# One wait taken out of the load queue of a hybrid attention and mixture-of-experts block

## The chip, the cores and the metric

The kernel runs on one core of a Trainium2 chip. The metric is the device time of one execution in microseconds; lower is better. Times inside an execution come from the hardware profiler and are counted from the start of its span.

## The reference

One transformer block on 512 tokens of width 2048, all in fp32. Three kinds of attention (differential, forgetting, and a compressed/selected/windowed one) are computed and projected by `w_out`, and the result is added to x. Then comes a hierarchical mixture of experts:

```python
g_prob = jax.nn.softmax((xt @ wg) + bg)                 # 8 groups
g_p, g_idx = lax.top_k(g_prob, 1)                       # one group per token
e_val, e_loc = lax.top_k(e_in, TOP_K_EXPERTS)           # 2 of the group's 8 experts
...
return (jax.nn.silu(xc @ w_gate[e]) * (xc @ w_up[e])) @ w_down[e]
...
x = x + hier_moe(h, ...)
return rms_norm(x, ln_f)
```

There are 64 experts; each has gate and up weights of 2048 x 256 and down weights of 256 x 2048, so three matrices of 2 MB (2048 KB) each, 384 MB (192 matrices) for all.

## The kernel before, in words

The first half of the execution is attention and the output projection. The sum x2 (x plus the attention's part) is stored to a scratch tensor in DRAM, transposed for the router, and the router's logits are made (`add_logits`, L1203).

The second half goes through the experts one by one, in 8 groups of 8. For a group the tokens that chose it are gathered as rows from the scratch tensor into `xg[g % 2]` by an indirect DMA that GpSimd issues (`gather`, L859; for the first group L865). VectorE builds a 0/1 matrix `pick` (L2170) that says which row goes to which slot of which expert, and TensorE multiplies the gathered rows by it (`pick_half`, L1285); ScalarE and VectorE copy the product to `xT`. The group's first four experts come from `pick_half(g, 0)`, the last four from `pick_half(g, 1)`. For each expert TensorE then runs `gate_up` (L1363 and L1364), a transpose (L1373), `down_product` (L1388) and `spread_result` (L1334), which adds the weighted result to the group's rows.

The weights come over SP's DMA queue (q1 in the profile). SP walks down a fixed list, `LOAD_ORDER`, and waits in front of each load for the buffer's last user. Load n has a number: 0 and 1 are gate and up of expert 0, 2 and 3 of expert 1, 4 is down of expert 0, 5 and 6 are gate and up of expert 2, 7 is down of expert 1, 8 is gate of expert 3, and so on. There are eight 16 KB-per-partition buffers that are used over and over (`chunk`). Load 6, the third expert's up weights, is alone: it is made once into two places of 8 KB per partition, `xg[1]` (where the second group's rows come later) and `lnf_sb` (where ln_f comes later), in two halves. Load 8 (L787) is issued ahead of load 6, and load 7 (L794) goes into the space of the transposed x2, so it waits for `logits_ready`. Loads 9 to 12 are made in quarters, each after TensorE's `gate_up` of expert 0 or 1 has read that quarter of the old contents (`load_quarters`, L747). From load 13 on each waits for TensorE to be done with the buffer (`chunk_used`, `load_chunk`, L734).

The gather is on GpSimd's own queue (q0 in the profile). TensorE's `pick_half(0, 0)` waits for both `pick_ready` and `xg_in[0]`, the gather's landing. Until then TensorE is kept busy by multiplications that nobody reads (`keep_busy`, L1240).

Of the kernel before, what the change touches and what calls it, by code (L numbers as in the profile page):

```python
# [351 lines left out]
def hybrid_block_moe_kernel(nc, x_in, ln1, w_in, diff_lambda, diff_subln, fox_bf, cmp_pos_k, cmp_w1_k,  # L352
# [3 lines left out]
    with ExitStack() as ctx:  # L356
# [6 lines left out]
        def sem(name):  # L363
            return ctx.enter_context(nc.semaphore(name))
# [246 lines left out]
        g_copied, xg_in, out_landed = sem("g_copied"), [sem(f"xg_in{b}") for b in range(2)], sem("out_landed")  # L611
# [45 lines left out]
        def _(sp):  # L657
# [73 lines left out]
            def load_chunk(n):  # L731
                e, kind = LOAD_ORDER[n]
                s = slot_of(n)
                sp.dma_start(chunk[s], sources[kind][:, e, :]).then_inc(ex_in[s], 16)  # L734
# [50 lines left out]
            sp.wait_ge(x2_transposed, 4 * NT)  # L785
            sp.wait_ge(row2_sum, NT * NT)
            load_chunk(SLOTS + len(ONCE) + 1)  # L787
            sp.wait_ge(xg_in[0], 16)
            for k in range(2):
                half = slice(k * KT // 2 * D_EXPERT, (k + 1) * KT // 2 * D_EXPERT)  # L790
                e, kind = LOAD_ORDER[ONCE[0]]
# [117 lines left out]
        def _(pe):  # L909
# [226 lines left out]
            for n in range(ALL_STEPS):  # L1136
                if n > 0:
                    fill(n, 0)
                fill_out(n)
                filled = any(lo < hi for _, lo, hi, _ in filling(n, 0))  # L1140
                if filled:
                    transpose_probs(n)
                if n >= 1:
                    values(n - 1)
                if not filled:
                    transpose_probs(n)
                fill(n, 1)
                if n + LOOK < ALL_STEPS:
                    scores(n + LOOK)
# [300 lines left out]
        def _(act):  # L1450
# [153 lines left out]
            def take_turns(n, half):  # L1604
                for tile, _, _, turns in filling(n, half):
                    if turns:
                        take_turned(tile)
# [14 lines left out]
            def turn_next(n):  # L1622
                return n < ALL_STEPS and any(turns and lo == KT for _, lo, _, turns in filling(n, 0))
# [741 lines left out]
```

## Time and profile before

| | us |
|---|---|
| median of 3 runs | 1950.96 |
| lowest and highest run | 1949.98, 1952.01 |
| span of the profiled execution, first to last instruction | 1948.3 |
| median less span | 2.7 |

| engine | busy us | share of the span |
|---|---|---|
| TensorE (PE) | 1871.1 | 96% |
| VectorE (DVE) | 702.2 | 36% |
| ScalarE (ACT) | 585.3 | 30% |
| GpSimd (POOL) | 245.5 | 13% |

The profile lists no separate time for the profiled execution; the 2.7 us are what lies between its span and the median of the runs. "Busy" counts an engine's own instructions; a DMA is seen in the columns for bytes per microsecond and in the time from its issue to its landing. A row of a timeline that ends with a bracket says how long the engine was idle before it and who released it.

### The profile page before, as it was taken

How to read it: one execution, taken by the hardware profiler on the slowest of the kernel's cores; microseconds unless marked ns; L12 is line 12 of the kernel's file. 1: busy time of each engine (PE TensorE's matmuls, PEld its weight loads, DVE VectorE, ACT ScalarE, POOL GpSimd, SP SyncE). 2: the span in 40 equal slices, each digit the busy share in tenths (PEclk: the TensorE clock that was granted, in tenths of full speed). 3: DMA queues.
4: the chain of work that ended last, by engine and by line, in shares of the span. 5: the costliest groups of instructions: out<-in, count | busy, mean ns of one | idle time of the engine just before them, and what ended most of it. 6: DMA issues, size and time to landing. Idle time of an engine off the chain costs nothing.

```text
span 1948.3 us, 28600 instructions
## 1 busy us (share of the span) xinstructions
PE 1871.1 (96%) x11936; PEld 1351.5 (69%) x11936; DVE 702.2 (36%) x1773; ACT 585.3 (30%) x1212; POOL 245.5 (13%) x208
## 2 busy tenths in 40 slices
PE   6999999999999999999999999989999899999996
PEld 5887777777777777788986656556565565655663
DVE  4331223333766668701142232322323123232322
ACT  5323333333543444422312231313213131121322
POOL 2433343333000000144100000000000000000000
PEclk9999999999999999999999999999999999999998
DMA  9553233233222231146499999999999999999994
GB/s 280 142 149 113 71 82 87 65 77 86 53 68 44 56 125 70 44 144 206 191 369 411 428 427 427 426 426 428 426 427 429 426 428 426 427 427 427 427 427 197
DMA packets 177393, 505.95 MB, mean 260 GB/s; under 512 B 52834, under 2 KB 136162, under 8 KB 151146
## 3 DMA queue, kind: packets, MB, share of 16 engines
q1 hardware_dynamic: 174954, 495.66, 66.4%
q0 software_dynamic: 2304, 8.39, 1.1%
q8 instruction: 97, 1.59, 0.3%
q14 instruction: 38, 0.31, 0.0%
HBM read 495.88 MB, written 16.53 MB: 263 GB/s over the span
## 4 chain that ended last, share of the span: by engine, by line
PE 79%; DMA 18%; ACT 1%; DVE 1%; issue 0%; SPq 0%; POOL 0%; POOLq 0%; ACTq 0%; DVEq 0%
PE banks L955 26%; PE banks L1363 12%; DMA at_region<-in_w_up 10%; PE banks L1112 9%; DMA x_region<-in_w_up 8%; PE banks L1388 7%; PE banks L1285 6%; PE banks L1364 3%; PE banks L1092 3%; PE banks L1064 2%; PE banks L1042 2%; PE banks L1334 2%; PE banks L1004 1%; PE banks L1203 1%; PE banks L1049 1%; PE banks L1373 1%
## 5 line engine op out<-in xcount | busy, mean ns | idle before, releaser
L955 PE MATMUL banks<-ht_rounded,ring_rounded 128*128 128x512 f32 x1056 | 359.3, 394 | 0.7 <-ACT at_region L1526 0.7
L955 PEld LDWEIGHTS banks<-ht_rounded,ring_rounded 128*128 128x128 f32 x1056 | 195.2, 188 | 53.5 <-issue 13.8
L1363 PE MATMUL banks<-at_region,ht_region 128*64 128x256 f32 x800 | 185.5, 392 | 13.3 <-DMA at_region<-in_w_up 13.3
L852 POOL TENSOR_TENSOR ring_rounded<-ring_region,at_rounded 128x512 fp32r<-128x512 f32 (+1 forms) x92 | 116.0, 1292 | 509.4 <-ACT at_rounded L1465 509.4
L1364 PE MATMUL banks<-at_region,ht_region 128*64 128x256 f32 x768 | 180.1, 395 | 0.0
L2257 DVE SCALAR_TENSOR_TENSOR at_rounded<-banks,small,ring_rounded 128x512 fp32r<-128x512 f32 x128 | 96.0, 750 | 208.4 <-ACT ring_rounded L1751 207.5
L1363 PEld LDWEIGHTS banks<-at_region,ht_region 128*64 128x64 f32 x800 | 112.1, 142 | 74.4 <-issue 27.7
L2250 DVE COPY consts<-banks 128x128 f32<-128x128 f32 x64 | 18.6, 291 | 397.9 <-PE banks L1373 397.9
L1751 ACT ACTIVATE ring_rounded<-banks,small 128x512 fp32r<-128x512 f32 x128 | 88.0, 688 | 240.1 <-PE banks L1388 240.1
L955 PE MATMUL banks<-ht_rounded,at_rounded 128*128 128x512 f32 x352 | 142.7, 405 | 1.0 <-ACT at_region L1518 0.7
L1741 ACT ACTIVATE ring_region<-banks,consts 64x256 f32<-64x256 f32 x64 | 30.1, 470 | 368.7 <-PE banks L1364 368.5
L955 PE MATMUL banks<-mix_rounded,at_rounded 128*128 128x512 f32 x352 | 137.6, 391 | 0.0
L955 PE MATMUL banks<-mix_rounded,ring_rounded 128*128 128x512 f32 x352 | 137.5, 391 | 0.0
L852 POOL TENSOR_TENSOR ring_rounded<-ring_region,ring_rounded 128x512 fp32r<-128x512 f32 x88 | 111.2, 1296 | 199.2 <-ACT ring_rounded L1465 199.2
L1112 PE MATMUL banks<-ring_rounded,ht_rounded 128*128 128x512 f32 x384 | 129.9, 392 | 0.0
L1285 PEld LDWEIGHTS banks<-ring_region,mix_region 128*128 128x128 f32 x512 | 116.7, 306 | 15.8 <-issue 12.2
L1285 PE MATMUL banks<-ring_region,mix_region 128*128 128x256 f32 x512 | 125.0, 399 | 0.0
L1363 PE MATMUL banks<-x_region,ht_region 128*64 128x256 f32 x480 | 107.9, 384 | 8.1 <-DMA x_region<-in_w_up 7.2
L1364 PE MATMUL banks<-x_region,ht_region 128*64 128x256 f32 x512 | 115.5, 384 | 0.0
L882 POOL DMA_INDIRECT out<-mix_region,g_idx x8 | 8.1, 1007 | 837.3 <-DVE mix_region L2267 837.3
L1364 PEld LDWEIGHTS banks<-at_region,ht_region 128*64 128x64 f32 x768 | 108.6, 143 | 0.0
L1363 PEld LDWEIGHTS banks<-x_region,ht_region 128*64 128x64 f32 x480 | 65.9, 138 | 45.6 <-issue 18.6
(300 smaller groups left out, 3473.7 us busy)
## 6 DMA issues: line engine op xcount, KB each, us to landing
at_region<-in_w_gate SPq DMA_DIRECT2D x24, 2048.0 KB, 29.8
at_region<-in_w_up SPq DMA_DIRECT2D x23, 2048.0 KB, 28.2
at_region<-in_w_down SPq DMA_DIRECT2D x22, 2048.0 KB, 24.4
ring_region<-in_w_in SPq DMA_DIRECT2D x36, 1024.0 KB, 6.0
x_region<-in_w_down SPq DMA_DIRECT2D x17, 2048.0 KB, 27.4
x_region<-in_w_up SPq DMA_DIRECT2D x15, 2048.0 KB, 30.0
x_region<-in_w_gate SPq DMA_DIRECT2D x14, 2048.0 KB, 30.2
ring_region<-in_w_gate SPq DMA_DIRECT2D x9, 2048.0 KB, 33.1
```

What stands on the lines that cost most here:

```text
L852: ins = nc.gpsimd.tensor_tensor(w_low[n % RING][:, ks, 0:width], ring[n % RING][:, ks, 0:width], w_high[n % 2][:, ks, 0:width].bitcast(F32 ...
L955: ins = mm(out, w[:, k, 0:width], h[:, k, :], start=k == 0 and i == 0, stop=k == KT - 1 and i == 2)
L1042: ins = mm(S[:, par, half, 0:W], q[pr][rows, cols], keys[kind == "win"][rows, 0:W], start=True, stop=True)
L1064: ins = nc.tensor.transpose(PT[:, half, kb * P:(kb + 1) * P], probs[:, n % 2, half, kb * P:(kb + 1) * P], ident)
L1092: ins = mm(o, v[:, kb, cols], pT[:, half, j * P:(j + 1) * P], start=kind == "fox" and kb == 0, stop=part != "slc" and kb == qb)
L1112: ins = mm(out, a[:, 4 * c + i, t * P:(t + 1) * P], b[:, i, :], start=first and i == 0 and k == 0, stop=last and i == 3 and k == 2)
L1285: mm(place[turn[j]][:, 0:HALF], rows[:, j, :], slots, start=True, stop=True).then_inc(picked, 1)
L1363: mm(place[0:CAP, 0:D_EXPERT], x, gate[j], start=j == 0, stop=j == KT - 1)
L1364: ins = mm(place[CAP:2 * CAP, 0:D_EXPERT], x, up[j], start=j == 0, stop=j == KT - 1)
L1388: ins = mm(PT[side * CAP:(side + 1) * CAP, m, :], hidT[:, j, :], down[:, j, (2 * side + m) * T:(2 * side + m + 1) * T], start=j == 0, stop ...
L1751: fn(y_high[:, m, :], PT[:, m, :], ACT.Copy, scale=own_weight[e8 % 2]).then_inc(y_a, 1)
L2257: v.scalar_tensor_tensor(y_low[:, m, :], PT[:, m, :], own_weight[e8 % 2], y_high[:, m, :].bitcast(F32), ALU.mult, ALU.subtract).then_inc(y ...
```

## The change

SP no longer waits for the landing of the first group's gathered rows (`xg_in[0]`) before it issues the two halves of load 6. Nothing else is changed.

```diff
             load_chunk(SLOTS + len(ONCE) + 1)
-            sp.wait_ge(xg_in[0], 16)
             for k in range(2):
                 half = slice(k * KT // 2 * D_EXPERT, (k + 1) * KT // 2 * D_EXPERT)
                 e, kind = LOAD_ORDER[ONCE[0]]
                 sp.dma_start(second_gate[k], sources[kind][:, e, half]).then_inc(once_in, 16)
             sp.wait_ge(logits_ready, 1)
             load_chunk(SLOTS + len(ONCE))
```

## Rows read from the trace of the kernel before

**Rows 1.** The page, chain of work that ended last, shares of the span.
```profile
PE 79%; DMA 18%; ACT 1%; DVE 1%; issue 0%; SPq 0%; POOL 0%; POOLq 0%; ACTq 0%; DVEq 0%
```

**Rows 2.** Stretches: length, then PE, PEld, DVE, ACT, POOL busy, clock, DMA share, GB/s.
```profile
982.00:986.00 4.00, 4.00 (x31) 3.96 (x30) 1.24 (x5) 0.47 (x1) 0.00 (x0) 1.00 0.34 86
...
1044.00:1051.00 7.00, 7.00 (x63) 4.68 (x64) 0.76 (x2) 0.47 (x1) 0.00 (x0) 1.00 1.00 424
1051.00:1054.00 3.00, 3.00 (x24) 1.52 (x22) 0.97 (x4) 0.47 (x1) 0.00 (x0) 1.00 0.66 213
1054.00:1224.00 170.00, 170.00 (x1222) 107.34 (x1220) 48.17 (x109) 40.19 (x74) 2.25 (x3) 1.00 1.01 427
1224.00:1926.00 702.00, 663.21 (x4644) 425.24 (x4642) 193.40 (x429) 163.04 (x300) 12.22 (x16) 0.98 1.00 424
```

**Rows 3.** The chain in order of time, second half: start us, us, what.
```profile
984.70 7.39 PE banks L1285 x32
...
1224.50 25.34 DMA at_region<-in_w_up
```

**Rows 4.** Waits of TensorE from 984 to 1220 us, all of them.
```profile
PE banks L1388 <- issue: 0.4, 1, 0.4
```

**Rows 5.** Timeline of SP's queue: start us, us, line, operation.
```profile
965.30 0.33 SPq L734 DMA_DIRECT2D mix_region<-in_w_gate  x1
984.15 0.33 SPq L792 DMA_DIRECT2D mix_region<-in_w_up  x1
...
985.00 0.43 SPq L734 DMA_DIRECT2D ht_region<-in_w_down  x1
994.94 0.33 SPq L747 DMA_DIRECT2D at_region<-in_w_up  x1
...
1051.75 0.33 SPq L734 DMA_DIRECT2D at_region<-in_w_down  x1
```

**Rows 6.** Timeline of all engines around the first gather.
```profile
972.44 0.19 DVE L2106 TENSOR_TENSOR at_region<-banks,small 128x32 f32<-128x32 f32 x1 [11.29 <-PE banks L1203]
...
978.76 1.17 POOL L865 DMA_INDIRECT mix_region<-x_scratch,idx_i  x1 [42.53 <-issue]
...
983.81 0.69 DVE L2170 TENSOR_TENSOR ring_region<-consts,small 128x512 f32<-128x512 f32 x1
...
984.55 7.54 PE L1285 MATMUL banks<-ring_region,mix_region 128*128 128x256 f32 x32
```

**Rows 7.** DMA view of 978 to 990, 1749 to 1763, 1940 to 1949 us.
```profile
q0 software_dynamic: 144, 0.44, 12.5%
...
mix_region<-x_scratch,idx_i POOLq DMA_INDIRECT x1, 5.4
...
q0 software_dynamic: 145, 0.16, 3.1%
...
mix_region<-x_scratch,g_idx POOLq DMA_INDIRECT x1, 10.3
...
q0 software_dynamic: 144, 0.16, 5.1%
...
out<-mix_region,g_idx POOLq DMA_INDIRECT x1, 3.8
```

**Rows 8.** DMA view of 986 to 990 and 1040 to 1050 us: packets by size.
```profile
DMA packets 205, 1.55 MB, mean 387 GB/s; under 512 B 16, under 2 KB 16, under 8 KB 16
...
DMA packets 292, 4.26 MB, mean 426 GB/s; under 512 B 32, under 2 KB 32, under 8 KB 32
```

**Rows 9.** TensorE after two idle times: timeline rows and stretches (columns as above).
```profile
1491.99 0.40 PE L1363 MATMUL banks<-mix_region,ht_region 128*64 128x256 f32 x1 [2.34 <-DMA at_region<-in_w_up]
...
1492.00:1495.00 3.00, 3.00 (x28) 2.44 (x30) 1.63 (x1) 0.00 (x0) 0.54 (x1) 1.00 1.03 437
...
1418.51 0.66 PE L1363 MATMUL banks<-at_region,ht_region 128*64 128x256 f32 x1 [2.49 <-DMA at_region<-in_w_up]
...
1418.40:1421.60 3.20, 3.09 (x16) 1.99 (x18) 0.00 (x0) 0.00 (x0) 0.00 (x0) 0.50 1.00 425
1421.80:1425.00 3.20, 3.20 (x32) 2.33 (x30) 0.00 (x0) 0.00 (x0) 0.00 (x0) 1.00 1.01 430
```

## The prediction, made before the changed kernel ran

> **What bounds the kernel now.** I read the page's chain first: 79% of the span on TensorE and 18% on DMA [rows 1]. Such shares are a mean over stages, so the next view is the table of stretches [rows 2]. From 1054 us almost to the end the DMA engines move 424 to 427 GB/s with no gap. From 1054 to 1224 us TensorE is busy for all of its 170 us as well; after 1224 us it is busy for 663 of 702 us and waits for weights. The chain says the same: it stays on TensorE from the first picking at 984.70 us until, at 1224.50 us, the first DMA stands in it [rows 3]. So the last 700 us go at the pace of the weight stream, and what matters is when that stream becomes unbroken, and who sets that moment.
>
> The stretches show it: from 1044 to 1051 us the stream runs at 424 GB/s, from 1051 to 1054 us only at 213 [rows 2]. SP's queue shows why: a load is issued at 1051.75 us [rows 5], for a buffer that TensorE has just freed, and the queue ahead of it had run dry. From there on it never does again. And TensorE, from 984 to 1220 us, has one wait of 0.4 us [rows 4]: it runs back to back from the first `pick_half`. Hence the rule that I use: **the end of the kernel moves by as much as TensorE's start on `pick_half(0, 0)` moves**. A transfer that arrives earlier between 984 and 1051 us only makes the dry moment before 1051.75 us longer.
>
> What releases that start at 984.55 us? Two things, almost at once [rows 5, 6]. VectorE's `pick` is done at 983.81 + 0.69 = 984.50 us. The gather was issued at 978.76 us and landed 5.4 us later [rows 7], at about 984.15 us, which is when SP, waiting for the same landing, went on [rows 5]. So the gather has only some 0.35 us of slack.
>
> **The change, part by part.** *What is moved.* SP had issued load 8 at 965.30 us and then stood until 984.15 us [rows 5]. Now the two halves of load 6 follow at about 965.7 and 966.1 us, 18.5 us earlier. Load 7, behind them on SP, waits only for the logits, which TensorE finishes as VectorE is released at 972.44 us [rows 6]; it goes out at about 972.5 instead of 985.00 us, 12.5 us earlier. Behind it come the quarters of loads 9 to 12; the first is issued at 994.94 us [rows 5] after `gate_up` of expert 0 has read its quarter, so they stay tied to TensorE. GpSimd's queue isn't changed: the gather is still issued at 978.76 us.
>
> *What is gained.* From 982 to 986 us the stream was almost empty, 86 GB/s [rows 2]: a hole of (427 - 86) x 4 = 1364 KB, 3.2 us of stream. It is now filled. By the rule above that buys nothing, since no one waits for loads 6 or 7 before 1051 us [rows 4]: they were in time already. Value: 0. If it did reach the end, it would be worth up to 3.2 + 0.9 (the ramp from 986 to 990 us at 387 GB/s, 160 KB or 0.4 us, and the hole's edges, about 0.5) = 4.1 us; that is the lower bound, and a rival below.
>
> *What is lost.* The gather used to travel as load 8 ran out. Now 4.2 MB more lie in SP's queue when it starts: 9.8 us at 427 GB/s, so the stream is full until about 992 us, beyond any time at which the gather could land. What does an indirect DMA cost beside a full stream? The nearest rows are two of one size, 0.16 MB each [rows 7]: alone, at the end of the kernel, 3.8 us; beside the stream, 10.3 us. The stream costs 6.5 us. The gather has 144 packets, 9 for each of the 16 engines. Packets of the stream are 16 KB where a row of 16 KB is loaded: from 1040 to 1050 us 292 less 32 small ones carry 4.26 MB, 16.4 KB each [rows 8], which at a sixteenth of 427 GB/s is 0.61 us. The 6.5 us are then 10.6 such packets: about one ahead of each of the gather's nine and one or two more at the start. But load 6 goes into two places of 8 KB per partition, and its packets are half as large: from 986 to 990 us 205 less 16 small ones carry 1.55 MB, 8.2 KB each [rows 8], 0.31 us. The gather meets the tail of load 8 and then load 6, which alone fills 4.9 us. So 10.6 x 0.31 = 3.3 us, plus 0.3 us for one packet of load 8 ahead of it. The gather itself, alone, with 0.44 MB: 3.8 + 0.28 MB / 427 GB/s = 4.5 us. Sum: 4.5 + 3.3 + 0.3 = 8.1 us, landing at 986.9 us. TensorE starts 2.4 us later than 984.55 us.
>
> The bounds of this term: below, 5.4 us as now, a delay of 0. Above, all of the stream priced as 16 KB packets: 10.3 + 0.7 = 11.0 us, landing at 989.8 us, a delay of 5.3 us. I take 2.4 us since the packets' size is what the rows say of this very load.
>
> The Trainium skill, in DMA: Bandwidth & Descriptors, "Queues, rings and completion order", says that each DMA engine goes round its queues and changes only at packet boundaries. By that alone, nine stream packets for nine of the gather's, the sum would be 4.5 + 9 x 0.31 = 7.3 us and the delay 1.6 us; no row here shows the order of single packets. The same page's fit in "Anatomy of one DMA", about 2 us plus the bytes at 436 GB/s, would price the gather at 3.0 us beside anything, and the change at nothing; the trace disagrees with 10.3 us for 0.16 MB.
>
> *TensorE's clock.* TensorE would now be idle for about 2.3 us between the end of its kept-busy work and `pick_half`. The trace has idle times on both sides of what that does [rows 9]: after 2.34 us the granted clock stayed at 1.00 (2.4 GHz); after 2.49 us it was 0.50 (1.2 GHz), and 16 matmuls ran in 3.2 us where 32 ran afterwards: 1.6 us lost. At 2.3 us I take it as not falling, 0, and keep 1.6 us for the range.
>
> *Everything else* follows TensorE and shifts with it: the marks on VectorE, the quarters, the second gather. The instructions removed cost nothing.
>
> Sum: 0 + 2.4 + 0 = **+2.4 us**; the span 1948.3 becomes 1950.7, and with the 2.7 us that the median lies above the span, **1953.4 us**. A measurement of this kernel can tell about 0.2% (3.9 us) from no change, so this is a loss that would count as none.
>
> **Rivals.** *A, the forecast with a fallen clock.* The same delay a little longer, and 1.6 us for the clock: 1950.96 + 2.4 + 1.6 = 1955.0 us, just past 0.2%. For it: 2.3 us of idling stands directly at 2.34 and 2.49 us. Against: the idle time is spread over only one row of each kind, and picking is also paced by copies.
>
> *B, the stream costs the gather its full price.* Packets already taken in by the engines, or load 7 being met as well, make it like the later gathers: 5.3 us of delay and 1.6 us of clock, 1957.9 us. For it: the smallest indirect DMA beside the stream took 10.3 us [rows 7]. Against: the 8 KB packets.
>
> *C, nothing happens.* The gather finishes nearly as fast as now, within its slack of 0.35 us or a microsecond of it: 1951.0 to 1952 us. For it: the present 5.4 us already contain over 2 us beside load 8. Against: 10.3 against 3.8 us.
>
> *D, faster.* The hole of up to 4.1 us is the weight stream's own time, and that stream sets the pace of the last 700 us. If the load at 1051.75 us were not tied to TensorE, or TensorE's start did not move and something before 1051 us was short of weights, the end would come up to 4.1 us earlier, 1946.9 us. It decides at the dry moment: the stream must be unbroken through 1051 to 1054 us. Against it: 213 GB/s there, and TensorE's single wait of 0.4 us [rows 2, 4].
>
> **How the numbers follow.** Forecast with the clock kept 0.40; A 0.22; B 0.17; C 0.13; D 0.08. The forecast's own range is 1952.3 to 1954.8 us. The range from C's 1951.0 less a microsecond of spread between runs to near B: 1950.0 to 1957.6 us. Slower by over 0.2% is B and most of A: 0.34. Faster by over 0.2% is D alone, at its full price: 0.07. The rest, 0.59, is the same.
>
> **What the changed profile would show.** SP issues the two halves near 965.7 us and load 7 near 972.5 us. No stretch from 978 to 990 us falls below 400 GB/s; the stream runs dry between about 992 us and the first quarter instead. The gather's time to landing is 8.1 us. TensorE has a wait for it in front of L1285 of about 2.3 us, with the clock beside it. The first quarter is issued near 997.3 us, and the load now at 1051.75 us near 1054.2 us, again with the stream dry before it. The prediction is wrong if L1285 starts on time, if the wait is over 4 us, or if the stream shows no gap near 1054 us.

## The result and the profile after

The changed kernel takes 1956.07 us (median of 10 runs, 1953.17 to 1957.19) against 1951.57 us for the kernel before in the same runs (1949.98 to 1952.74). The ratio is 1.0022, with a 95% interval from 1.0013 to 1.0031: 4.3 us slower, and the interval excludes no change. It lies in the predicted range of 1950.0 to 1957.6 us; the predicted step was 2.4 us, and the line of 0.2% on which the chances were cut runs through the measured interval, so whether the loss is above or below it isn't decided.

The profiled execution took 1956.5 us, with a span of 1954.6 us. All that lies ahead of the router came about 1.1 us later in it than in the profile of before (the gather is issued at 979.83 instead of 978.76 us), which has nothing to do with the change. So times are best read as distances from the issue of the gather. The lines of `kernel.py` behind the removed one have moved up by one: L1284 here is L1285 of before.

SP's queue, the rows that answer to [rows 5] (start us, us, line, operation):

```profile
966.35 0.33 SPq L734 DMA_DIRECT2D mix_region<-in_w_gate  x1
966.72 0.43 SPq L791 DMA_DIRECT2D mix_region<-in_w_up  x1
...
973.41 0.33 SPq L734 DMA_DIRECT2D ht_region<-in_w_down  x1
1001.34 0.33 SPq L747 DMA_DIRECT2D at_region<-in_w_up  x1
...
1058.15 0.33 SPq L734 DMA_DIRECT2D at_region<-in_w_down  x1
```

Load 6 follows load 8 at once, and load 7 went out with the logits. But the first quarter and the load that was at 1051.75 us are later, not earlier.

Stretches of the changed kernel (columns as in [rows 2]):

```profile
982.00:986.00 4.00, 3.77 (x42) 3.57 (x42) 2.16 (x7) 0.20 (x1) 0.00 (x0) 1.00 1.01 412
986.00:990.00 4.00, 0.64 (x3) 0.67 (x4) 0.00 (x0) 0.00 (x0) 0.00 (x0) 1.00 1.05 434
...
994.00:996.00 2.00, 2.00 (x10) 2.00 (x10) 1.18 (x3) 0.95 (x2) 0.00 (x0) 1.00 0.00 0
996.00:998.00 2.00, 2.00 (x10) 2.00 (x10) 1.15 (x3) 0.95 (x2) 0.00 (x0) 1.00 0.00 0
998.00:1000.00 2.00, 2.00 (x26) 1.77 (x26) 1.54 (x4) 0.47 (x1) 0.00 (x0) 1.00 0.00 0
...
1057.00:1060.00 3.00, 3.00 (x26) 1.66 (x24) 0.97 (x4) 0.47 (x1) 0.00 (x0) 1.00 0.91 333
```

The hole of before, 86 GB/s from 982 to 986 us, is filled: 412 GB/s. It has come back at 994 to 1000 us, where nothing moves at all. In its place TensorE is idle from 985.8 to 989.4 us. The dry moment in front of the later load is still there, at 1057 to 1060 us, but it is shallower: over the three microseconds that begin 0.75 us ahead of that load's issue the stream runs at 317 GB/s, against 213 before [rows 2].

The one of TensorE's waits from 940 to 1400 us that lies in front of the first picking, then the chain that ended last, in order of time (start us, us, what), and TensorE's stretches right after its wait:

```profile
PE banks L1284 <- DMA mix_region<-x_scratch,idx_i: 3.6, 1, 3.6
```

```profile
979.83 9.40 DMA mix_region<-x_scratch,idx_i
...
989.36 9.12 PE banks L1284 x32
```

```profile
990.30:993.60 3.30, 3.30 (x10) 2.58 (x9) 0.97 (x2) 1.03 (x3) 0.00 (x0) 0.50 0.69 293
993.70:997.00 3.30, 3.30 (x17) 3.30 (x16) 1.77 (x4) 1.60 (x4) 0.00 (x0) 1.00 0.01 5
```

The gather, 5.4 us long before [rows 7], takes 9.4 us and is now in the chain. TensorE waits 3.6 us for it. While the granted clock is at 0.50, 10 matmuls run in 3.3 us instead of 17, and the first picking takes 9.12 instead of 7.39 us [rows 3]. From the gather's issue to the later load it is 1058.15 - 979.83 = 78.32 us, against 1051.75 - 978.76 = 72.99 us before [rows 5, 6]: 5.3 us more. That is 9.12 - 7.39 = 1.7 us for the clock and 3.6 us for the later start. Behind the later load nothing is won or lost again in this execution: from its issue to the end of the span it is 1954.6 - 1058.15 = 896.5 us, against 1948.3 - 1051.75 = 896.6 us before.

### The profile page after: what moved, and what is told of

Same layout as the page of the kernel before. It is cut to its first block, busy times and chain, and to the rows that moved or that the text cites. A ratio compares the mean times of both kernels' runs of the same rounds, so it can differ in the third digit from the quotient of the medians.

```text
span 1954.6 us, 28600 instructions
## 1 busy us (share of the span) xinstructions
PE 1875.4 (96%) x11936; PEld 1353.7 (69%) x11936; DVE 706.5 (36%) x1773; ACT 584.7 (30%) x1212; POOL 245.3 (13%) x208
## 4 chain that ended last, share of the span: by engine, by line
PE 79%; DMA 18%; ACT 1%; DVE 1%; issue 1%; SPq 0%; POOL 0%; POOLq 0%; ACTq 0%; DVEq 0%
PE banks L954 25%; PE banks L1362 12%; DMA at_region<-in_w_up 10%; PE banks L1111 9%; DMA x_region<-in_w_up 7%; PE banks L1387 7%; PE banks L1284 6%; PE banks L1363 3%; PE banks L1091 3%; PE banks L1063 2%; PE banks L1041 2%; PE banks L1333 2%; PE banks L1003 1%; PE banks L1202 1%; PE banks L1048 1%; PE banks L1372 1%
## 5 line engine op out<-in xcount | busy, mean ns | idle before, releaser
L1284 PEld LDWEIGHTS banks<-ring_region,mix_region 128*128 128x128 f32 x512 | 117.6, 306 | 20.2 <-issue 15.9
L1284 PE MATMUL banks<-ring_region,mix_region 128*128 128x256 f32 x512 | 126.6, 403 | 3.6 <-DMA mix_region<-x_scratch,idx_i 3.6
```

The lines of the kernel that those rows point to most:

```text
L1284: mm(place[turn[j]][:, 0:HALF], rows[:, j, :], slots, start=True, stop=True).then_inc(picked, 1)
```

## Experiments

Each was timed against the kernel before on the same chip. The table gives, from the profile of each, the gather's time to landing, TensorE's wait in front of the first picking, the length of that picking, and the distance from the gather's issue to the load that was at 1051.75 us. The last column is timed, the others are one execution each.

| kernel | landing | wait | picking | to the load | ratio (95%) |
|---|---|---|---|---|---|
| before | 5.4 | 0 | 7.39 | 72.99 | 1 |
| changed | 9.4 | 3.6 | 9.12 | 78.32 | 1.0022 (1.0013 to 1.0031) |
| load 7 alone early | 10.3 | 3.2 | 9.14 | 79.27 | 1.0027 (1.0018 to 1.0036) |
| load 6 alone early | 9.3 | 3.6 | 8.90 | 78.03 | 1.0022 (1.0013 to 1.0031) |
| changed, TensorE kept warm | 9.4 | 0.9 | 7.51 | 76.70 | 1.0012 (1.0003 to 1.0021) |
| before, late start | 5.4 | 0 | 7.27 | 79.58 | 1.0035 (1.0023 to 1.0047) |
| wait for the gather's issue | 8.1 | 2.3 | 9.14 | 77.06 | 1.0012 (1.0003 to 1.0021) |
| loads 6, 7 later | 5.4 | 0 | 7.38 | 74.30 | 1.0014 (1.0005 to 1.0023) |
| loads 6, 7 much later | 5.3 | 0 | 7.38 | 72.94 | 1.0024 (1.0015 to 1.0033) |

The timed ratios have intervals of about 1.8 us on either side, so small differences between kernels are read from the profiles, and what reaches the end from the ratios. A profile is of one of the timed executions and need not be a typical one: for the wait for the gather's issue and for both kernels with later loads it is the slowest of eleven. What is seen at the later load is carried on at first: the load that was at 1243.26 us before is still 5.4 us later in the changed kernel and 6.6 us later after the late start. Further on the clock and TensorE's waits for weights fall differently in each execution, and the distance wanders by up to 3.5 us.

**Which load hurts the gather.** Load 7 alone ahead of the wait (`...` marks what is left out, the comments are added here):

```diff
-            sp.wait_ge(xg_in[0], 16)
-            for k in range(2):                      # load 6
-                ...
             sp.wait_ge(logits_ready, 1)
             load_chunk(SLOTS + len(ONCE))           # load 7
+            sp.wait_ge(xg_in[0], 16)
+            for k in range(2):                      # load 6
+                ...
```

> Only load 7 is moved ahead of the wait for the gather, load 6 stays behind it. Theory (the gather's packets take turns with the stream's, so the stream's packet size sets the delay): load 7 has 16 KB packets, so the gather lands about 10.5 us after its issue, later than the 9.4 us beside load 6; TensorE's wait before the first picking is about 4.7 us, the clock falls, and the end is some 6 us later than the kernel before (ratio 1.003). The stream has only 2 MB extra, gone by about 987 us, which may end the competition a little early: then 9.5 us. Rival (any full queue costs the same, whatever is in it): 9.4 us as after the change, and the same time as the changed kernel (ratio 1.0022).

And load 6 alone, the order of the changed kernel with the wait put between the two loads:

```diff
-            sp.wait_ge(xg_in[0], 16)
             for k in range(2):                      # load 6
                 ...
+            sp.wait_ge(xg_in[0], 16)
             sp.wait_ge(logits_ready, 1)
             load_chunk(SLOTS + len(ONCE))           # load 7
```

> Only load 6 is moved ahead, load 7 waits for the gather. Theory (load 6 alone does the harm): the gather lands 8.5 to 9.4 us after its issue, TensorE waits 2.7 to 3.6 us, the clock falls in about half of the executions, and the end is 3 to 5 us later than before (ratio 1.0015 to 1.0025). Rival (load 7, with the larger packets, does the harm): landing at 5.4 to 6.5 us, no wait over 1 us, ratio 1.0000 to 1.0005.

The gather in the chain, of load 7 alone and then of load 6 alone:

```profile
980.25 10.33 DMA mix_region<-x_scratch,idx_i
```

```profile
979.10 9.33 DMA mix_region<-x_scratch,idx_i
```

Either load is enough: 10.3 and 9.3 us. For load 6 alone the landing, the wait (3.6 us) and the end (4.3 us later) are as its theory had them. For load 7 alone the wait of 3.2 us is shorter than the 4.7 us expected, but the picking does start 4.5 us later, counted from the gather: the kept-busy work ahead of it had met a granted clock of 0.50 from 979 to 982 us and ended 1.3 us late. The end is 5.3 us later, where 6 were expected.

The DMA view splits the landing times. The first answer of each pair is the time in which no packet of q0 moved at all, the second the rest, with all 144. For load 7 alone, 980.25 to 984.5 us and 984.5 to 990 us:

```profile
DMA packets 129, 1.84 MB, mean 434 GB/s; under 512 B 16, under 2 KB 16, under 8 KB 16
...
DMA packets 223, 1.47 MB, mean 268 GB/s; under 512 B 106, under 2 KB 106, under 8 KB 106
...
q0 software_dynamic: 144, 0.44, 20.0%
```

For the changed kernel, 979.83 to 984.1 us and 984.1 to 988.8 us:

```profile
DMA packets 189, 1.76 MB, mean 412 GB/s; under 512 B 21, under 2 KB 21, under 8 KB 21
...
DMA packets 333, 2.03 MB, mean 432 GB/s; under 512 B 115, under 2 KB 115, under 8 KB 115
...
q0 software_dynamic: 144, 0.44, 23.6%
```

In both the gather stood for some 4.3 us before its first packet. In the kernel before no packet of q0 moved from 978.76 to 980.7 us, 1.9 us. That first part grew by 2.3 us whichever load was ahead. Only the rest depends on the load: 10.3 - 4.3 = 6.0 us to the landing beside packets of 16 KB, 9.4 - 4.3 = 5.1 us beside mostly smaller ones, 5.4 - 1.9 = 3.5 us before the change. So the theory's direction is right, larger packets cost more, but packet size is worth 1 us here and not 3. That 1 us is no full price: in the rest the engines moved 432 GB/s in the changed kernel but only 268 with load 7 alone, whose 2 MB of extra stream were running out, and a stream of 16 KB packets that stays full was not tried on this gather. The rival's flat 9.4 us is excluded only by that 1 us, by one execution with load 7 alone against three with load 6 ahead (9.40, 9.33, and 9.39 us in the next experiment).

**The clock.** The changed kernel with TensorE kept busy longer:

```diff
             place_slots(0)
-            keep_busy(6)
+            keep_busy(18)
```

> The changed kernel with 12 more multiplications that nobody reads ahead of the first picking, 3.1 us of work at 0.26 us each, which fill most of TensorE's wait of 3.6 us. Theory (the delay is the late landing plus 1.7 us for the fallen clock): the first picking starts as in the changed kernel, its 32 rows take 7.5 instead of 9.1 us at a granted clock of 1.00, and the end is 1.7 us earlier than the changed kernel's slower executions: about +3.5 us on the kernel before (ratio 1.0018), with less spread between executions. Rival (the clock's loss is taken up later, before the weight stream becomes the bound): the time of the changed kernel, ratio 1.0022 or more.

The landing is the same 9.4 us, and the wait is 0.9 us:

```profile
988.60:992.00 3.40, 3.40 (x15) 3.40 (x16) 1.39 (x3) 1.43 (x3) 0.00 (x0) 1.00 0.91 386
```

15 matmuls in 3.4 us at a granted clock of 1.00, against 10 in 3.3 us at 0.50 in the changed kernel; the first picking takes 7.51 us. The distance to the later load is 1.6 us shorter than in the changed kernel. The ratio, 1.0012, is on the theory's side of 1.0018, but its interval overlaps the changed kernel's; the timing alone doesn't prove the clock's share. The profile does, as far as the later load: there the rival's taking up of the loss hasn't happened. The prediction of less spread failed: 1950.53 to 1956.26 us.

**Does the end move with TensorE's start?** The kernel before, with no DMA touched and 30 more useless multiplications:

```diff
             place_slots(0)
-            keep_busy(6)
+            keep_busy(36)
```

> The kernel before, with its wait in place and no DMA moved, but with 30 more such multiplications ahead of the first picking: TensorE is busy and the picking starts 7.8 us later, near 992.4 us. Theory (the end moves by as much as the first picking): +7.8 us, 1959.4 us, ratio 1.0040; the load before was at 1051.75 us comes 7.8 us later with the stream dry before it. Rival (the weight stream alone sets the end, and TensorE's lead of 240 us takes the delay up): +0 to 2 us, ratio 1.0000 to 1.0010.

The 30 took 6.6 instead of 7.8 us, and the distance to the later load grew by as much, 79.58 - 72.99 = 6.6 us. The stream was dry again in front of that load:

```profile
1060.00:1063.00 3.00, 3.00 (x22) 1.47 (x20) 0.97 (x4) 0.47 (x1) 0.00 (x0) 1.00 0.67 175
```

The end moved by 6.8 us (ratio 1.0035, 4.5 to 9.2 us). The rival's 0 to 2 us is excluded: TensorE's lead over the weights doesn't take the delay up.

**Filling the hole behind the gather.** SP waits until GpSimd has issued the gather (`g_copied` is counted by the instruction behind it), not until it has landed:

```diff
-            sp.wait_ge(xg_in[0], 16)
+            sp.wait_ge(g_copied, 1)
```

> The kernel before, but SP waits only until GpSimd has issued the first gather, not until it has landed. Loads 6 and 7 go out at about 980.3 instead of 984.2 us, when the gather's packets are already in their queue. Theory (what counts is how much of the stream is queued when the gather arrives; filling the hole in the stream buys nothing): the gather lands 6 to 7 us after its issue, TensorE waits 0.3 to 1.3 us with the clock unchanged, and the end is 0.3 to 1.3 us later than before (ratio 1.0002 to 1.0007). Rival (a filled hole is time gained for a kernel that is bound by its weight stream): 2 to 4 us earlier, ratio 0.998 to 0.999.

```profile
981.28 1.18 POOL L865 DMA_INDIRECT mix_region<-x_scratch,idx_i  x1 [42.55 <-issue]
```

```profile
982.73 0.33 SPq L792 DMA_DIRECT2D mix_region<-in_w_up  x1
```

```profile
989.53 4.80 PE L1285 MATMUL banks<-ring_region,mix_region 128*128 128x256 f32 x13 [2.34 <-DMA mix_region<-x_scratch,idx_i]
```

The expectation missed. Load 6 was issued 1.45 us after the gather and still made it 8.1 us long. The gather's first part was short (no q0 packet from 981.28 to 983.2 us, as before the change), but the rest, 8.1 - 1.9 = 6.2 us, was as long as beside a full stream. TensorE waited 2.34 us, the granted clock was 0.50 from 991.5 to 993.5 us, and the picking ran 9.14 us. The later load comes 77.06 - 72.99 = 4.1 us later in this profile. At 1.0012, 2.3 us (0.6 to 4.1), the kernel is slower than the one before, and the rival's gain did not come. The profiled execution, 1956.91 us, is the slowest of eleven and 4.2 us above their median, so the gather may be less late in the others; the timing alone doesn't exclude the expected 0.3 to 1.3 us.

**Has the stream slack?** The other way round: loads 6 and 7 later, with gather and TensorE untouched.

```diff
-            sp.wait_ge(xg_in[0], 16)
+            sp.wait_ge(picked, 8)
```

> The kernel before, but SP waits for the eighth product of the first picking instead of the gather, so that loads 6 and 7 go out some 4 us later, near 988.2 us, and the hole in the stream from 982 us on is 4 us longer. Gather and TensorE are untouched. Theory (between 984 and 1051 us the weight stream has slack of its own: 2.2 us of ramp at the first quarters and 1.5 us at the dry moment, 3.7 us together): the stream runs through both places, TensorE waits for nothing, and the end is 0 to 0.5 us later (ratio 1.0000 to 1.0003). Rival (the stream sets the end and every microsecond of it that is lost or won counts): +4 us, ratio 1.0021; then filling the hole would also have been worth its 3 to 4 us and the loss by the gather would be larger than it looks.

In the profiled execution the first picking began 1.3 us later than it should, behind kept-busy work that had met a low clock, so load 6 went out 5.7 us later than before, counted from the gather (991.25 - 980.20 = 11.05 us against 984.15 - 978.76 = 5.39 us). The measured 1.0014 is 2.7 us: more than the expected 0.5, less than the rival's 4, and it decides nothing. Hence once more, with all sixteen products waited for:

```diff
-            sp.wait_ge(xg_in[0], 16)
+            sp.wait_ge(picked, 16)
```

> As the run before it with loads 6 and 7 made later, but SP waits for all 16 products of the first picking: they go out near 991.9 us, 7.8 us later than in the kernel before. That run left 1.0014 between two theories; twice the delay sets them further apart. Theory (the stream has 3.7 us of slack of its own between 984 and 1054 us, and only what goes beyond that reaches the end): 7.8 - 3.7 = 4.1 us later, ratio 1.0021, with the stream at over 420 GB/s all through 1050 to 1060 us and TensorE waiting for weights before 1220 us. Rival (each microsecond of the stream counts): 7.8 us, ratio 1.0040.

```profile
994.77 0.33 SPq L792 DMA_DIRECT2D mix_region<-in_w_up  x1
...
1054.40 0.33 SPq L734 DMA_DIRECT2D at_region<-in_w_down  x1
```

```profile
988.00:994.00 6.00, 6.00 (x29) 6.00 (x28) 3.02 (x7) 3.32 (x7) 0.00 (x0) 1.00 0.00 0
...
1050.00:1054.00 4.00, 4.00 (x42) 2.61 (x38) 0.00 (x0) 0.00 (x0) 0.00 (x0) 1.00 1.01 426
1054.00:1058.00 4.00, 4.00 (x26) 1.82 (x24) 0.97 (x4) 0.77 (x2) 0.00 (x0) 1.00 0.98 418
```

```profile
PE banks L1363 <- DMA x_region<-in_w_up: 2.6, 1, 2.6
PE banks L1363 <- DMA at_region<-in_w_up: 0.9, 1, 0.9
```

Counted from the gather (981.46 us), load 6 is 13.31 - 5.39 = 7.9 us later, and TensorE is where it was: 72.94 us to the later load. The dry moment is gone, 426 and 418 GB/s through it, and TensorE already waits for weights between 984 and 1220 us (the two waits above). The end moved by 4.7 us (1.0024, 2.9 to 6.4 us): 7.9 less the slack of 3.7 is 4.2, and the rival's 7.8 is outside. That there is slack is shown; its size is less sure, 1.5 to 5.0 us by the interval. So a stream that comes later costs only what exceeds its slack. That one that comes earlier, with TensorE where it is, has nothing to gain follows from the same reading, but no run here shows it by itself: wherever loads 6 and 7 went out earlier, TensorE was late too.

**The dry moment itself.** The kernel before, with loads 19 and 20 in quarters like loads 9 to 12:

```diff
-QUARTERED = ((9, 10), (11, 12))
+QUARTERED = ((9, 10), (11, 12), (19, 20))
+QUARTER_USERS = (0, 1, 4)
...
-                            sp.wait_ge(quarter_used, 3 * e_before + k + 1)
+                            sp.wait_ge(quarter_used, 3 * QUARTER_USERS.index(e_before) + k + 1)
...
-            for n in range(QUARTERED[-1][-1] + 1, CHUNKS - 3):
+            for n in range(QUARTERED[1][-1] + 1, CHUNKS - 3):
+                if n == QUARTERED[2][0]:
+                    load_quarters(QUARTERED[2])
+                if n in QUARTERED[2]:
+                    continue
...
-                    if begins_all(c, g) and e8 < len(QUARTERED) and j % 4 == 3 and j < KT - 1:
+                    if begins_all(c, g) and e8 in QUARTER_USERS and j % 4 == 3 and j < KT - 1:
```

> The kernel before, wait in place; loads 19 and 20, which went out at 1051.75 us into a dry stream, are now made in quarters, each after TensorE's reading of that quarter by the gate and up product of expert 4. Theory (the weight stream is broken there by TensorE and by nothing else, and sets the end from there on): their first pieces go out some 5 us earlier, 1051 to 1054 us no longer falls to 213 GB/s, and the end comes 1.5 us earlier (ratio 0.9992), which is near what can be told. Rival (the dry moment costs nothing, TensorE sets the end): the stream is filled and the time is that of the kernel before.

> The kernel of the run with loads 19 and 20 in quarters once more, beside other runs of the kernel before, since its first ratio of 0.9995 (0.9986 to 1.0004) decides nothing. Theory: 1.0 to 1.5 us earlier than before, ratio 0.9992 to 0.9995 again. Rival: 1.0000, and what was seen was spread.

```profile
1048.31 0.33 SPq L748 DMA_DIRECT2D at_region<-in_w_down  x1
```

```profile
1051.00:1054.00 3.00, 3.00 (x31) 1.92 (x29) 0.13 (x1) 0.47 (x1) 0.00 (x0) 1.00 0.93 388
1054.00:1057.00 3.00, 3.00 (x19) 1.18 (x17) 0.84 (x4) 0.22 (x1) 0.00 (x0) 1.00 1.01 406
```

The first time the ratio was 0.9995 (0.9986 to 1.0004), the second 0.9990 (0.9981 to 0.9999). The rows, of the second, show the first piece issued 5.2 us earlier, counted from the gather, and the stream at 388 and 406 GB/s where it fell to 213. The mean of the two, 0.9992 or 1.5 us, is what was expected, and only the second interval excludes no change, so the rival (the dry moment costs nothing) is made unlikely and not more. It is the one version here that came out ahead of both kernels, by very little.

## Why the prediction came out as it did

**What bounds the kernel** was right. The end follows the first picking: 6.6 us of late start with no DMA touched gave 6.8 us. The stream's slack ahead of 1054 us is real too: 7.9 us of later loads gave 4.7 us. One sentence was wrong: the earlier loads did not make the dry moment longer. It became shorter, 317 instead of 213 GB/s, because the hole now lies in front of the first quarter: the quarters start with an empty queue, are done later in relation to TensorE, and reach closer to the later load. That last link is read from the rows and was not tested.

**What is moved** was right. Load 6 went out at 966.72 us and load 7 at 973.41 us, which is 965.7 and 972.3 us on the clock of the kernel before, where 965.7 and 972.5 were forecast. The hole moved behind them to 994 us. Only 377 GB/s from 980 to 982 us falls below the 400 that the forecast had for every stretch there.

**What is gained**, value 0, agrees with the runs: 3.2 us of hole filled, the later load not earlier, and the time behind it unchanged at 896.5 us. Rival D, the gain, found nothing on its side.

**What is lost** had the right cause and was too small: 8.1 us forecast for the gather, 9.4 us measured; 2.4 us of delay forecast for the picking, 3.6 us of wait measured. The term that was mis-sized is "10.6 x 0.31 = 3.3 us, plus 0.3 us for one packet of load 8". With the prediction's own 4.5 us for the gather alone, it measured 9.4 - 4.5 = 4.9 us instead of 3.6. It halved the whole of the 6.5 us that a full stream costs. But 2.3 us of what is lost come ahead of the gather's first packet and are the same with load 7 alone, where the stream's packets are larger. The 4.5 us are no firm base: the 3.8 us in them are of a store to `out`, not of a gather, and no run has this gather without a stream; as the stream ran out it took 5.4 us. The section's upper bound of 11.0 us, all of it at 16 KB, was not reached either: load 7 alone gave 10.3 us, beside a stream that ran out.

The rule of the Trainium skill that engines take turns between queues at packet boundaries (DMA: Bandwidth & Descriptors, "Queues, rings and completion order") would have made it 7.3 us. The runs agree with it in one thing, that the part after the first packet takes longer beside larger packets, 6.0 against 5.1 us. They go beyond it in another: by the rule alone the first packet would stand behind one packet of the stream, and it came 2.3 us later than before. What counts as a packet in the profile may also not be what the page calls one; no run here shows it.

**The clock** was taken as not falling at a wait of 2.3 us. The wait was 3.6 us, and it fell: 1.7 us, where 1.6 was kept for the range. So the profiled execution is rival A with a longer delay: 3.6 + 1.7 = 5.3 us, between A's 4.0 and B's 6.9. Over all runs the end moved by 4.3 us. That this is so near A's 4.0 is partly luck, since A had the delay 1.2 us too small. Whether the three quickest of the ten runs, 1953.2 to 1953.7 us, are those in which the clock held can't be told from their times and stays open.

## What to carry to other kernels

A load that is issued early into an idle stretch of a queue isn't free if something small and urgent is about to use the same DMA engines: here 2 MB of weights that TensorE first multiplies with at 1013.0 us of the kernel before made a 0.44 MB gather 4 us late. Before moving a load, ask which transfer lands just in time beside it, and how many microseconds it can spare; here it was 0.35. In a kernel bound by its weight stream, a hole in the stream is worth filling only behind the last moment at which a compute engine breaks the stream. Here that is an inference: filling the dry moment itself gave 1.5 us as the mean of two measurements, near what can be told from none.

## What was not expected of the hardware

- A load issued 1.45 us after an indirect DMA still slowed it from 5.4 to 8.1 us. Being issued first gave the gather no right of way.
- The gather needed 4.3 us to its first packet beside a full stream, against 1.9 us where the stream was running out. The 4.3 us were the same whether the stream's packets ahead of it were larger or smaller, on the average 1.82 MB / 127 = 14.3 KB (load 7 alone) or 1.74 MB / 187 = 9.3 KB (the changed kernel).
- A TensorE wait of 2.34 us was followed by a granted clock of 0.50 in one kernel (the wait for the gather's issue, picking 9.14 us) and left it at 1.00 in another place of the kernel before [rows 9]. In the profiles of load 7 alone, of the loads made later and of the first one with quarters the clock fell to 0.50 near 979 us, though TensorE's only wait from 940 to 980 us was one of 0.5 us, as in the kernel before, where it stayed at 1.00. The length of one idle time alone doesn't say what the clock will do.
